# Closing the experts' sum at expert 13, and gating the last two experts when they are evicted

## The reference

```
for l in range(2):
    mod = silu(c) @ ada_w[l] + ada_b[l]          # g2: its last 1024 columns, one gate per feature
    x = x + g1 * token_mix(...)
    h = rmsnorm(x, norm2_g[l]) * (1 + sc2) + sh2
    x = x + g2 * grouped_moe(h, ...)             # 16 experts, 2 of them for each token
return rmsnorm(x, final_g)

# grouped_moe: y = sum over e of combine[:, e] * ((silu(h @ w_gate[e]) * (h @ w_up[e])) @ w_down[e])
```

## Time and profile before

| | us |
|---|---|
| median of three runs | 1593.18 |
| lowest and highest run | 1592.16, 1597.57 |
| the profiled execution, whole | 1596.89 |
| its span, first to last instruction | 1595.1 |
| PE busy in it | 1442.3 (90%) |
| DVE busy | 955.2 (60%) |
| ACT busy | 670.9 (42%) |

### The profile page before, as it was taken

One profiled execution on the slowest core, in us unless ns is written; L12 is line 12 of the kernel. 1 busy time (PEld: TensorE's weight loads), 2 busy tenths in 40 slices (PEclk: granted clock), 3 DMA queues, 4 the chain that ended last, 5 costly groups with the idle time before them and its releaser, 6 DMA issues.

```text
span 1595.1 us, 27221 instructions
## 1 busy us (share of the span) xinstructions
PE 1442.3 (90%) x10760; PEld 1173.7 (74%) x10760; DVE 955.2 (60%) x1482; ACT 670.9 (42%) x1065; POOL 43.5 (3%) x99
## 2 busy tenths in 40 slices
PE   6999999699999899998899989969999889899994
PEld 6899989459999797986556666649789765566663
DVE  5888857658888744788624443344478853434342
ACT  5444444544444553554234433334355422443331
POOL 3300000000000000000100000000000020000000
PEclk9999999799999899999899999979999989999997
DMA  9899775056999655323269999985533334999995
GB/s 322 285 346 351 272 226 185 1 184 223 351 335 329 211 155 166 109 103 106 106 244 392 413 394 385 391 309 174 153 127 106 106 112 197 409 403 398 394 388 216
DMA packets 159793, 401.96 MB, mean 252 GB/s; under 512 B 6410, under 2 KB 102396, under 8 KB 143324
## 3 DMA queue, kind: packets, MB, share of 16 engines
q1 hardware_dynamic: 158768, 398.81, 68.8%
q10 hardware_dynamic: 380, 1.08, 0.3%
q0 software_dynamic: 560, 0.88, 0.2%
HBM read 399.70 MB, written 1.05 MB: 251 GB/s over the span
## 4 chain that ended last, share of the span: by engine, by line
PE 73%; DVE 14%; ACT 6%; DMA 5%; issue 3%; ACTq 0%; DVEq 0%; SPq 0%
PE bank L1432 14%; PE bank L1311 8%; PE bank L1508 7%; PE bank L1444 6%; PE bank L1516 6%; PE bank L1299 6%; PE bank L1334 5%; PE bank L1567 3%; DMA sb_ring<-in_w_up 3%; PE bank L1360 3%; PE bank L1556 2%; DMA sb_ring<-in_w_gate 2%; PE bank L1582 2%; DVE sb_w_lo L2270 1%; DVE sb_w_lo L2175 1%
## 5 line engine op out<-in xcount | busy, mean ns | idle before, releaser
L1432 PE MATMUL bank<-sb_hT_hi,sb_w_hi 128*128 128x256 f32 x704 | 198.3, 282 | 4.2 <-DVE sb_hT_lo L2152 3.1
L1432 PE MATMUL bank<-sb_hT_lo,sb_w_hi 128*128 128x256 f32 x704 | 196.7, 279 | 0.0
L1432 PE MATMUL bank<-sb_hT_hi,sb_w_lo 128*128 128x256 f32 x704 | 196.4, 279 | 0.0
L2196 DVE TENSOR_TENSOR sb_w_lo<-sb_ring,sb_w_hi 128x1024 fp32r<-128x1024 f32 x128 | 151.2, 1223 | 61.4 <-ACT sb_w_hi L818 61.3
L818 ACT ACTIVATE sb_w_hi<-sb_ring 128x1024 fp32r<-128x1024 f32 x128 | 128.9, 1056 | 115.3 <-PE bank L1432 114.9
L2175 DVE TENSOR_TENSOR sb_w_lo<-sb_ring,sb_proj_hi 128x1024 fp32r<-128x1024 f32 x100 | 117.9, 1220 | 62.3 <-ACT sb_proj_hi L798 62.1
L1508 PE MATMUL bank<-sb_ring,sb_arena 128*32 128x128 f32 (+1 forms) x2304 | 140.4, 321 | 6.7 <-DMA sb_ring<-in_w_gate 5.0
L1432 PEld LDWEIGHTS bank<-sb_hT_hi,sb_w_hi 128*128 128x128 f32 x704 | 132.4, 188 | 6.0 <-issue 4.9
L1311 PE MATMUL bank<-sb_w_lo,sb_hT_hi 128*128 128x256 f32 x480 | 134.8, 281 | 0.0
L1432 PEld LDWEIGHTS bank<-sb_hT_lo,sb_w_hi 128*128 128x128 f32 x704 | 133.4, 189 | 0.7
L798 ACT ACTIVATE sb_proj_hi<-sb_ring 128x1024 fp32r<-128x1024 f32 x100 | 101.0, 1064 | 77.9 <-PE bank L1299 35.0
(11 more groups left out here) (549 smaller groups left out, 2960.5 us busy)
## 6 DMA issues: line engine op xcount, KB each, us to landing
sb_ring<-in_w_up SPq DMA_DIRECT2D x64, 1024.0 KB, 7.4
sb_ring<-in_w_gate SPq DMA_DIRECT2D x64, 1024.0 KB, 7.4
sb_ring<-in_w_down SPq DMA_DIRECT2D x64, 1024.0 KB, 7.9
sb_ring<-in_w_in SPq DMA_DIRECT2D x46, 1024.0 KB, 5.3
sb_ring<-in_ffn_w_in SPq DMA_DIRECT2D x44, 1024.0 KB, 9.2
sb_arena<-in_ada_w SPq DMA_DIRECT2D x32, 1280.0 KB, 6.9
sb_ring<-in_ffn_w_out SPq DMA_DIRECT2D x22, 1024.0 KB, 8.2
sb_ring<-in_w_out SPq DMA_DIRECT2D x12, 1024.0 KB, 4.9
```

The costliest lines, as they stand in the source:

```text
L1432: ins = mm(bank[4 + 2 * p + b][:, jj * SEQ:(jj + 1) * SEQ], w[wp][:, k, jj * P:(jj + 1) * P], h_parts[hp][:, k, :], start=k == 0 and m == ...
L2196: ins = tt(w_lo[:, slot, c], ring[:, slot, c], w_hi[:, q % 2, c].bitcast(F32), ALU.subtract)
```

## The change

At position 14 the sum is cut in two. `acc` is closed with the scatter of position 13 (`group_ends`). DVE multiplies its four quarters by `gbc` into `xn`, and later adds `xn` to x, both while expert 15 runs. The scatter of position 14 opens a new group in `acc` and waits for those multiplications. The down products of positions 14 and 15 are no longer evicted by ACT but by DVE, which multiplies them by the gate as it reads them (`ye_gated`); so what `acc` holds at the end needs no gate and `add_whole_to_x` is one addition a quarter.

For that the gate is needed in the quarters' layout, `gate_quarters`, 128 partitions by 256. At the router PE makes it in bank 0 with four matmuls of 32 weight columns, in place of two of the four `keep_clock` matmuls behind the counts, and ACT copies it. PE waits for the copy ahead of its branch. The semaphores scores, counts and combine are merged with new ones into `router_act`, `router_pe` and `weighed`. The branch for tokens that don't fit (not taken with these inputs) multiplies the banks in place.

```diff
 # ACT, at the router
-                A(rt[:, 0, :], bank[2][:, 0:T * NE], ACT.Sigmoid).then_inc(s["scores"], 1)
+                A(rt[:, 0, :], bank[2][:, 0:T * NE], ACT.Sigmoid).then_inc(s["router_act"], 1)
+                act.wait_ge(s["router_pe"], 2 * run)
+                A(gate_quarters[:, :], bank[0][:, 0:SEQ], ACT.Copy).then_inc(s["router_act"], 1)
                 act.wait_ge(s["fits"], run)
 # ACT, experts
                 def quarter(e, i=0):
-                    ye_high(e - 1, i)
                     if e < NE - 1:
+                        ye_high(e - 1, i)
                         window(e + 1, i)
...
                 quarter(15)
-                ye_high(15)
 # PE, experts
-                expert(14)
-                expert(15)
+                expert(14, group_ends=True)
+                rows("u0", 15, bank[5], 0)
+                weights(15)
+                down(14)
+                gate_up(15)
+                pe.wait_ge(s["weighed"], 3 * l + 2)
+                scatter(14, first=True)
+                turn_hidden(15)
                 down(NE - 1)
                 scatter(NE - 1, last=True)
 # PE, at the router
-                keep_clock(4)
+                keep_clock(2)
+                for c in range(4):
+                    ins = mm(bank[0][c * QUART:(c + 1) * QUART, 0:SEQ], ones[:, 0:QUART], diag[:, 2 * c:2 * c + 2, :], start=True, stop=True)
+                ins.then_inc(s["router_pe"], 1)
                 pe.wait_ge(s["fits"], run)
-                pe.wait_ge(s["combine"], run)
+                pe.wait_ge(s["router_act"], 2 * run)
+                pe.wait_ge(s["weighed"], 3 * l + 1)
 # DVE, experts
+                def ye_gated(e):
+                    v.wait_ge(s["router_act"], 2 * l + 2)
+                    v.wait_ge(tiles_used, pos0 + tile_of("d1", e) + 1)
+                    v.wait_ge(s["scattered"], NE * l + e)
+                    tt(ye_quarter, bank[6][:, 0:SEQ], gate_quarters[:, :], M).then_inc(s["ye_hi"], 1)
...
                 quarter(14)
-                quarter(15)
-                puts(NE - 1)
+                v.wait_ge(s["scattered"], NE * l + 14)
+                for n, (t, half) in enumerate(QUARTERS):
+                    ins = tt(xn[:, t, half * 512:(half + 1) * 512], acc[n][:, :], gbc[:, half * 512:(half + 1) * 512], M)
+                ins.then_inc(s["weighed"], 1)
+                weights(15)
+                puts(14)
+                v.wait_ge(s["weighed"], 3 * l + 2)
+                for t, half in QUARTERS:
+                    c = slice(half * 512, (half + 1) * 512)
+                    ins = tt(x[:, t, c], x[:, t, c], xn[:, t, c], AD)
+                ins.then_inc(s["weighed"], 1)
+                ye_gated(14)
+                product(15)
+                puts(15)
+                ye_gated(15)
 # DVE, end of the layer
+            def add_whole_to_x():
+                for t, half in ((0, 0), (0, 1), (1, 0), (1, 1)):
+                    if t and half:
+                        mean_square(0)
+                    quarter_done()
+                    c = slice(half * 512, (half + 1) * 512)
+                    tt(x[:, t, c], x[:, t, c], acc[2 * t + half][:, :], AD).then_inc(s["x"], 1)
...
-                add_gated_to_x(quarter_done)
+                v.wait_ge(s["weighed"], 3 * run)
+                add_whole_to_x()
```

More of the change, by code:

```diff
@@ L124, in build @@
         quarter_col = by_slot[:, 6:7]
+        gate_quarters = sb("gate_quarters", [P, SEQ])
         arena_at = nc.sbuf_base
@@ L285, in build @@
         acc = bank[0:4]
+        QUARTERS = ((0, 0), (0, 1), (1, 0), (1, 1))
         IN_BANK = [bank[n] for n in (4, 5, 0, 1, 2, 3, 6, 7)]
@@ L421, in build @@
             act=(("xg_act", KC // 2), ("moe_hi", 12 * len(WIDE)), ("pick_own", NE - 1),
[L422 removed]
+                 ("wide_in", len(WIDE)), ("narrow_in", len(NARROW)), ("m_silu", NE), ("m_hid_hi", NE), ("ye_hi", NE - 2), ("pos_out", NE // 2)),
             pe=(("gathered", KC), ("pos_turned", 2), ("pos_bc", NE // 2), ("w_psum", NE), ("m_hidT", NE), ("scattered", NE), ("put_round", len(QUARTER))),
             v=(("xg_dve", KC // 2), ("moe_lo", 6 * len(WIDE)), ("wide_lo", len(WIDE)), ("posT", 4), ("w_slot", NE),
[L425 removed]
+               ("m_prod", NE), ("m_hid_lo", len(WIDE)), ("put", NE), ("ye_lo", len(WIDE)), ("ye_hi", 2)))
         def tile_of(kind, e):
@@ L1248, in _ @@
             PARTS = ((0, 0), (0, 1), (1, 0))
-            QUARTERS = ((0, 0), (0, 1), (1, 0), (1, 1))
             turns = [0]
@@ L1582, in scatter @@
                                     ins = mm(acc[2 * t + half][:, n * SEQ:(n + 1) * SEQ], put_narrow[c * QUART:(c + 1) * QUART, t * P:(t + 1) * P],
-                                             ye_quarter[c * QUART:(c + 1) * QUART, :], start=first, stop=last and n == 1)
+                                             ye_quarter[c * QUART:(c + 1) * QUART, :], start=first and n == 0, stop=last and n == 1)
                                     if last and n == 1 and (t, half) != QUARTERS[-1]:
@@ L1625, in gate_up, with expert @@
                     rows("u1", e, bank[5], 1, i)
-                def expert(e, i=0):
+                def expert(e, i=0, group_ends=False):
                     rows("u0", e, bank[5], 0, i)
@@ L1632, in expert @@
                     gate_up(e, i)
-                    scatter(e - 1, i)
+                    scatter(e - 1, i, last=group_ends)
                     turn_hidden(e, i)
@@ L2009, in _ @@
                 mm(bank[1][:, 2 * NE:3 * NE], ones[:, :], member[:, NE:2 * NE], start=False, stop=True, skip_group_check=True)\
-                    .then_inc(s["counts"], 1)
-                keep_clock(4)
+                    .then_inc(s["router_pe"], 1)
+                keep_clock(2)
+                for c in range(4):
+                    ins = mm(bank[0][c * QUART:(c + 1) * QUART, 0:SEQ], ones[:, 0:QUART], diag[:, 2 * c:2 * c + 2, :], start=True, stop=True)
+                ins.then_inc(s["router_pe"], 1)
                 pe.wait_ge(s["fits"], run)
-                pe.wait_ge(s["combine"], run)
+                pe.wait_ge(s["router_act"], 2 * run)
+                pe.wait_ge(s["weighed"], 3 * l + 1)
                 fits_ = pe.value_load(fits[0:1, 0:1], min_val=0, max_val=1)
@@ L2863, in _ @@
                 cp(small_a[:, 0, 0:SEQ], bank[3][:, 0:SEQ]).then_inc(s["logit_rows"], 1)
-                v.wait_ge(s["scores"], run)
+                v.wait_ge(s["router_act"], 2 * l + 1)
                 v.wait_ge(s["slot_patterns"], run)
@@ L2908, in _ @@
                 link(v.reciprocal(mx, mx))
-                tt(r(15), r(13), mx.unsqueeze(2).broadcast_to([P, T, NE]), M).then_inc(s["combine"], 1)
-                v.wait_ge(s["counts"], run)
+                tt(r(15), r(13), mx.unsqueeze(2).broadcast_to([P, T, NE]), M).then_inc(s["weighed"], 1)
+                v.wait_ge(s["router_pe"], 2 * l + 1)
                 rows3 = lambda z: z.rearrange("p (t e) -> p t e", t=T)
@@ L2965, in _ @@
                     every_token(l)
+                    for q in range(4):
+                        c = slice(q % 2 * 512, (q % 2 + 1) * 512)
+                        ins = tt(acc[q][:, :], acc[q][:, :], gbc[:, c], M)
+                    ins.then_inc(s["weighed"], 1)
+                    v.sem_inc(s["weighed"], 1)
                     if l < LAYERS - 1:
```

## The result

The changed kernel is slower: median 1604.09 us against 1595.01 for the kernel before, 22 runs of each; the ratio is 1.0045, with an interval of 1.0030 to 1.0061, some 7 us. It is an estimate over the single runs; the two medians alone lie 9.1 us apart. Forecast were 1590.6 and a range up to 1595.0; the fourth rival gave slower 0.07, and by another cause.

What follows compares the result with a forecast made beforehand. The weight stream was taken to bound the experts, and a single file of PE, ACT and DVE steps the end. Terms -2.5 - 1.6 + 1.7 + 0 = -2.4 us took the median from 1593.2 to 1590.8, given as 1590.6; range 1586.0 to 1595.0.

Steps and rivals of the forecast that it cites:

- the fourth rival: Both routers: the clock stays low over the whole of both gathers, +10.9 us in sum, 1604; chance 0.07.
- The step that failed: Router: DVE's chain sets the gather's start and ACT's copy is in time; 0, or up to +0.3 us in layer 1.
- The clock at the gather: Router, layer 0: PE idle 3.9 us drops the clock under the gather, +1.7 us; layer 1 no loss, bound 1.7.
- The third rival: Both gathers pay for the clock, or layer 0's end gain is lost: -0.7 or -0.8 us, 1592.4; chance 0.21.
- When the quarters come: Router: ACT's copy of the gate's quarters is done near 798 in layer 0 and 1324.5 in layer 1.
- The ends of the layers: Last additions to x: one addition a quarter brings ACT's scaled copy earlier, -2.5 us in layer 1, -1.6 in layer 0.
- The insertions at experts 14 and 15: DVE's added multiplications, additions and evictions in the experts' loop are hidden: 0, bounds -0.1 and +0.2 us.

Runs made afterwards that it cites:

- the run with one bare wait: Kernel before, with PE also waiting for DVE's pick ahead of its read of fits and the branch: 1608.78 us, ratio 1.0062.
- the swapped branches: Changed kernel with PE's two branches in the other order, the sparse path right behind the branch instruction: 1599.48 us, ratio 1.0018.
- the run with the router part alone: Kernel before, with two keepers, the four quarter matmuls, ACT's unused copy and PE's wait for it ahead of the branch: 1608.49 us, ratio 1.0059.
- The run with early quarters: Changed kernel with quarter matmuls behind PE's turn of the rows, copy before ACT's sigmoid, four keepers, no copy wait before the branch: 1594.55 us, ratio 0.9969.

## Why the prediction was wrong, point by point

**The step that failed.** "So DVE's chain, not PE, sets the gather, and the copy on ACT (done near 798 and 1324.5) is in time: 0, or up to +0.3 in layer 1." The 1.0 us from the pick to the gather was a coincidence of two routers whose DVE steps have the same lengths: fits leads the pick by the same time in both, so a constant distance to the one is a constant distance to the other. What set the gather was PE's own passage through the branch, 4.5 us from its last wait, which before was fits. The copy took the place of fits and was 3.7 us later in layer 0 (796.71 to 800.37) and 2.9 in layer 1. Measured: +4.2 and +2.8 us where 0 was put down, 0.6 of the 4.2 being the late fits; the run with one bare wait and the swapped branches show the cause. The timeline had the hint: 2.46 us idle in one layer and 0.73 in the other, in the earlier trace rows, the one ascribed to DVE and the other to "issue". A row of "issue" ahead of the first instruction behind a branch should have been priced.

**The clock at the gather: a real cost, too small, and its reason half right.** 1.7 us in one layer was forecast; it was 2.4 and 2.6 in two. With PE idle 4.9 us the clock fell in both (1.00 at 800 to 802, 0.81 at 802 to 804), and it stayed at half under the first six pairs of the gather's sixteen. The run with two keepers prices it without the wait: +3.1 and +2.4 in counts to order. But it also had half clock behind a gap of 2.28 us, shorter than the 2.46 from which the prediction read that the clock holds; its two keepers had run wholly at half clock, where four had brought the clock back. The third rival had both gathers pay; at its 3.4 us the sum would still have been -0.7.

**When the quarters come.** The copy was put at 798 in layer 0, 3.6 us behind the last step ahead of the counts. It ended 6.77 behind it, at 800.37, because the clock was at half under the keepers (3.76 us for four records) in this execution; at full clock, in the run with the router part alone, it ended 3.92 behind it, at 797.93. That is worth up to 2.9 us of lateness and depends on the execution. Even the early copy did not come in time: in that run the gather started 8.64 us behind the last step ahead of the counts, where it was 7.08 before.

**The ends of the layers: right.** 2.57 and 1.63 were worked out, 2.59 and 1.63 measured, each step included: the fourth addition behind the mean, ACT's L800 between its squares. The run with early quarters turns them into time.

**The insertions at experts 14 and 15: right.** Timeline of the changed kernel:

```profile
1564.18 2.48 DVE L2388 TENSOR_TENSOR sb_xn<-bank,sb_gbc 128x512 f32<-128x512 f32 x4 [1.45 <-PE bank L1600]
...
1566.58 0.15 DVE L2298 COPY sb_by_slot<-bank 128x1 f32<-128x1 f32 x1
...
1569.39 0.42 DVE L2327 TENSOR_TENSOR sb_arena<-bank,sb_gate_quarters 128x256 f32<-128x256 f32 x1
...
1570.79 1.56 PE L1509 MATMUL bank<-sb_ring,sb_arena 128*32 128x128 f32 x32 [1.52 <-DMA sb_ring<-in_w_gate]
```

The slot weights' copy waits behind the four multiplications, and w_gate still releases the next matmul 4.2 us behind it, as in the earlier trace rows. `ye_gated` takes the 0.42 forecast, and the hand-over to the last scatter is 0.70 of PE's idle time where it was 0.60: +0.1.

## What to carry to other kernels

A wait that stands ahead of a branch on TensorE delays more than itself: the jump to far code (here 3.7 to 5.1 us from the last wait to the first matmul) starts only then, so put such a wait behind the branch, at the instruction that needs it, or make its producer earlier. Before a wait is called free, ask what ended the idle time at the same place in each repetition; a distance that is the same in two layers doesn't say which of two equally spaced events caused it. Where PE must idle short of a dense burst, a few queued matmuls without a use can pay: 5.0 us at the router by the traces. At the end of the weight stream they gave 2 to 4 us by the ratios (0.9969 to 0.9955, and 0.9976 alone), which is at the edge of what these runs can tell.

## What the runs showed of the hardware that was not expected

- PE's branch to code past a long unused path takes 3.71 and 4.03 us to the first matmul; with the used path next to it the gather starts 1.06 us behind the last wait, if nothing else holds it. Queued matmuls hide it: ten keeper records ran through nearly the whole of the jump (799.81 to 804.34, the gather at 804.58).
- Swapping the two paths only moves the jump: behind the experts PE's first turn then came 2.93 and 2.50 us behind the start of ACT's scaled copy (0.54 without the swap), and once another 4.30 us stood between two transposes of one straight sequence. PE had been idle for 6.8 us ahead of the first turn in both. Weight transfers were moving some 350 GB/s there, where at the router next to none did; whether that lengthens a jump was not run.
- The idle time right ahead of the gather doesn't tell its clock: behind 4.9 us it was at half (2.4 and 2.6 us lost), behind 2.46 us with four keepers ahead at full, but behind 2.28 and 2.12 us with two keepers ahead at half again (the run with two keepers, layer 0, and the one with the wait inside the gather, layer 1).
- At the last weight tiles, with idle stretches of 1.3, 1.5, 0.9 and 0.6 us between bursts of 1.1 to 1.9 us, the clock fell in the changed kernel's profiled execution (0.62 at 1571 to 1572) and was still at half when the last scatter ended at 1591.2. In the kernel before, with 1.4, 1.5, 1.1 and 0.6 us, it fell too (0.77 at 1565 to 1566) and was back seven us later.

Left open: why the turn of the rows stood still a second time in the run with swapped branches, though its 4.30 us are in the sum above; whether a taken branch over a short path is cheap; and what decides between two executions of one kernel whether the clock comes back at the last weight tiles. Nothing was run to tell these.
